# A decoder layer on one core: a ninth slot for expert weights in two halves, and the final gain as one row

## What is computed

```python
def hierarchical_moe(x, g_ffn, w_rg, b_rg, w_re, b_re, w_gate, w_up, w_down):
    xn = rmsnorm(x, g_ffn)
    ...                        # one of 4 groups, then two of its 8 experts, weights in combine
    for g in range(N_EXPERT_GROUPS):
        h = jax.nn.silu(jnp.einsum('nd,edf->nef', xn, w_gate[g])) * jnp.einsum('nd,edf->nef', xn, w_up[g])
        out = out + jnp.einsum('nef,efd->nd', h * combine[:, g, :, None], w_down[g])
    return x + out.reshape(bsz, L, D_MODEL)
...
y_prompt = rmsnorm(h_p, g_final)
y_sample = rmsnorm(h_s, g_final)
```

## Time and profile before

| | us |
|---|---|
| median of 3 runs | 1639.19 |
| lowest and highest of them | 1638.49, 1640.21 |
| the profiled execution, its time | 1643.52 |
| its span, first to last instruction | 1641.7 |
| TensorE busy | 1427.6 (87%) |
| VectorE busy | 531.2 (32%) |
| ScalarE busy | 408.4 (25%) |
| DMA, mean over the span | 332 GB/s, 545.72 MB |

### The profile page before, as it was taken

How to read it: one execution, slowest core, us unless ns; L and a number is a source line. 1 busy time by engine, 2 the same in 40 slices (tenths; PEclk the granted TensorE clock), 3 DMA queues, 4 the chain that set the end, 5 groups by cost and what they waited for, 6 DMA issues and landing times.

```text
span 1641.7 us, 24240 instructions
## 1 busy us (share of the span) xinstructions
PE 1427.6 (87%) x9959; PEld 939.8 (57%) x9959; DVE 531.2 (32%) x840; ACT 408.4 (25%) x684; POOL 26.6 (2%) x48
## 2 busy tenths in 40 slices
PE   7999999999999999998886887877867869958966
PEld 7999999999999999963231321322312412412411
DVE  5547775554455555531110111111111001101103
ACT  6444344333333334420201101101102002002003
POOL 0200020000000000000000000000000000000000
PEclk9999999999999999999898888799889797989979
DMA  8776555555555458589999999999999999999997
GB/s 335 295 259 253 155 161 184 184 184 182 184 179 179 179 217 336 218 308 428 427 429 428 427 429 428 428 428 428 427 428 427 429 428 428 428 429 427 430 428 315
DMA packets 51867, 545.72 MB, mean 332 GB/s; under 512 B 6160, under 2 KB 6208, under 8 KB 11480
## 3 DMA queue, kind: packets, MB, share of 16 engines
q1 hardware_dynamic: 50288, 540.30, 81.2%
q0 software_dynamic: 1392, 4.78, 1.0%
q10 hardware_dynamic: 144, 0.02, 0.0%
HBM read 541.34 MB, written 3.68 MB: 332 GB/s over the span
## 4 chain that ended last, share of the span: by engine, by line
PE 54%; DMA 41%; DVE 2%; ACT 1%; issue 1%; SPq 0%; DVEq 0%; ACTq 0%
DMA side<-in_expert_chunks 23%; DMA ring<-in_expert_chunks 15%; PE bank L1401 11%; PE bank L1402 11%; PE bank L1403 11%; PE bank L1760 8%; PE bank L1669 6%; DMA ring<-in_dense_units 3%; PE bank L1763 2%; PE bank L1697 1%; DVE w_lo L889 1%; ACT w_hi L622 1%; PE bank L1712 0%; PE bank L1563 0%; DMA trunk<-in_mem_cols 0%
## 5 line engine op out<-in xcount | busy, mean ns | idle before, releaser
L889 DVE TENSOR_TENSOR w_lo<-ring,w_hi 128x1024 fp32r<-128x1024 f32 x220 | 259.7, 1221 | 221.5 <-ACT w_hi L622 221.0
L1401 PE MATMUL bank<-xn_hi,w_hi 128*128 128x264 f32 x1120 | 319.8, 286 | 1.6 <-DVE w_lo L889 1.6
L1402 PE MATMUL bank<-xn_lo,w_hi 128*128 128x264 f32 x1120 | 318.1, 284 | 0.0
L1403 PE MATMUL bank<-xn_hi,w_lo 128*128 128x264 f32 x1120 | 317.8, 284 | 0.0
L622 ACT ACTIVATE w_hi<-ring 128x1024 fp32r<-128x1024 f32 x220 | 221.1, 1052 | 371.4 <-PE bank L1403 337.1
L1401 PEld LDWEIGHTS bank<-xn_hi,w_hi 128*128 128x128 f32 x1120 | 211.6, 189 | 3.0 <-issue 1.7
L1402 PEld LDWEIGHTS bank<-xn_lo,w_hi 128*128 128x128 f32 x1120 | 211.8, 189 | 0.1
L1403 PEld LDWEIGHTS bank<-xn_hi,w_lo 128*128 128x128 f32 x1120 | 210.7, 188 | 0.0
L1760 PE MATMUL bank<-ring,trunk 128*32 128x512 f32 x1024 | 144.7, 691 | 64.0 <-DMA ring<-in_expert_chunks 64.0
L1760 PE MATMUL bank<-side,trunk 128*32 128x512 f32 x768 | 122.5, 770 | 58.9 <-DMA side<-in_expert_chunks 58.8
L1669 PEld LDWEIGHTS bank<-trunk,x_all 128*128 128x128 f32 (+1 forms) x780 | 120.4, 211 | 90.0 <-issue 69.4
(11 more groups left out here) (308 smaller groups left out, 1624.4 us busy)
## 6 DMA issues: line engine op xcount, KB each, us to landing
ring<-in_expert_chunks SPq DMA_DIRECT2D x88, 2048.0 KB, 35.6
side<-in_expert_chunks SPq DMA_DIRECT2D x72, 2048.0 KB, 35.5
ring<-in_dense_units SPq DMA_DIRECT2D x109, 1024.0 KB, 4.8
trunk<-in_expert_chunks SPq DMA_DIRECT2D x24, 2048.0 KB, 35.4
ring<-in_expert_chunks SPq DMA_DIRECT2D x16, 1024.0 KB, 34.9
x_all<-in_k_cols SPq DMA_DIRECT2D x8, 512.0 KB, 8.1
x_all<-in_cache_mem_v SPq DMA_DIRECT2D x8, 512.0 KB, 6.7
x_all<-in_x_cols SPq DMA_DIRECT2D x1, 2112.0 KB, 12.1
```

The lines of the kernel that those rows point to most:

```text
L889: V.tensor_tensor(w_lo[n % 2][:, js, :], raw[n % 2][:, js, :], w_hi[n % 2][:, js, :], ALU.subtract).then_inc(lo_done, 1)
L1401: mm(ps[:, 0:n], w_hi[b][:, j, :], x_hi[:, j, :], start=j == k0, stop=False)
L1402: mm(ps[:, 0:n], w_hi[b][:, j, :], x_lo[:, j, :], start=False, stop=False)
L1403: ins = mm(ps[:, 0:n], w_lo[b][:, j, :], x_hi[:, j, :], start=False, stop=j == k1 - 1)
```

## The change

- **A ninth slot.** It consists of two halves in places that were free or have been freed: the place of the broadcast `g_final`, and 2048 words where `y` was. Chunks 14 and 23 of every round go there, each in two loads of 1 MiB. The other slots keep their chunks, but for two: chunk 15 goes to the slot of chunk 6, and chunk 22 to the slot of chunk 7.
- **The order of the loads.** A table `REFILL` says which chunk is loaded when chunk p has been used. In a round the queue now reads 8 to 13, 15, 22, 16 to 21, 23 in halves, then for the next round 6, 0 to 5, 7, and 14 in halves. Before, it read 8 to 23 and then 0 to 7.
- **Ahead of the loop** both halves of chunk 14 are loaded as well, the first where `g_final` was loaded, the second once the router's logits have been folded.
- **`g_final`** is loaded as one row of 8 KiB into partition 64 of the sample rows' tile, early in the output projection. TensorE spreads it to all partitions by a product with a matrix that has one row of ones (`final_gain`): ahead of chunk 17 into bank 0, ahead of chunk 19 into bank 1, ahead of chunk 23 into bank 6, between the halves of chunk 23 into bank 7, in every round. At the end VectorE multiplies from the banks (9 operations of 512 columns in place of 3 of 1536) and copies bank 7 once.
- **`y`** has two buffers of 512 columns in place of four; h is made in place.
- **Sample rows.** The product that puts their last 512 columns in bank 4 uses a shifted identity. It moves from behind the first gather to a place among the busy matmuls, of which two go.

```diff
+SLOT = [EORDER[c % 8] for c in range(CPR)]
+SLOT[14], SLOT[15], SLOT[22], SLOT[23] = 8, SLOT[6], SLOT[7], 8
+REFILL = ([(p, p + 8, 0) for p in range(6)] + [(6, 15, 0), (7, 22, 0)] + [(p, p + 8, 0) for p in range(8, 14)] +
+          [(14, 23, 0), (15, 6, 1)] + [(p, p - 16, 1) for p in range(16, 22)] + [(22, 7, 1), (23, 14, 1)])
...
+        nine_halves = [view(trunk, CHUNK + 2 * D, CHUNK // 2), view(side, 0, CHUNK // 2)]
...
+                    if k == 2:
+                        sp.wait_ge(x_zero, 1)
+                        sp.dma_start(g_row, g_final.rearrange("(o n) -> o n", o=1)).then_inc(gfin_in, 16)
...
-            sp.dma_start(gfin, g_final.rearrange("(o n) -> o n", o=1).to_broadcast([P, D])).then_inc(gfin_in, 16)
+            half_load(14, 0, slice(0, 1))
+            sp.wait_ge(aux_ready, A_LT + 1)
+            half_load(14, 1, slice(0, 1))
...
-            dve.wait_ge(gfin_in, 16)
-            for t, (p0, p1, _, _) in enumerate(ACC):
-                link(V.tensor_tensor(acc(t, 0, 1536), acc(t, 0, 1536), gfin[p0:p1, 0:1536], ALU.mult))
+            for q, signal in ((0, gf_ready), (1, gf_ready), (6, gf2_ready)):
+                dve.wait_ge(signal, npass * ROUNDS)
+                c0 = 512 * min(q, 2)
+                for t, (p0, p1, _, _) in enumerate(ACC):
+                    ins = V.tensor_tensor(acc(t, c0, c0 + 512), acc(t, c0, c0 + 512), bank[q][p0:p1, :], ALU.mult)
+            dve.wait_ge(gf3_ready, npass * ROUNDS)
+            link(V.tensor_copy(g_last, bank[7][:, :]))
...
+                    def final_gain(q, b):
+
+                        return mm(bank[b][:, :], spread_g, x[:, 2, q * 512:(q + 1) * 512], start=True, stop=True)
...
+                        if c == 17:
+                            final_gain(0, 0)
                         if c == 21:
                             last_columns(1)
+                        if c == 19:
+                            final_gain(1, 1).then_inc(gf_ready, 1)
+                        if c == CPR - 1:
+                            pe.wait_ge(aux_done, it * JPR + (A_E + JOB_S[2] + 3))
+                            final_gain(2, 6).then_inc(gf2_ready, 1)
...
                             if jj and c == CPR - 1:
                                 last_columns(2)
+                                final_gain(3, 7).then_inc(gf3_ready, 1)
                                 pe.wait_ge(half_full, it * 16 + 16)
```

More of the change, by code:

```diff
@@ L162, in branch_kernel @@
         fold = view(side, 6 * T, LG)
-        sq_rows = view(side, 7 * T, 3, P)
+        sq_rows = view(side, 6 * T + LG, 3, P)
         at = 4096
@@ L226, in branch_kernel, with weights @@
                   6: view(trunk, 0, CHUNK), 7: view(side, 12544, CHUNK)}
-        y = view(side, 0, 4, 512)
-        hs = view(side, 2048, 512)
-        h = view(side, 2560, 4, P)
+        nine_halves = [view(trunk, CHUNK + 2 * D, CHUNK // 2), view(side, 0, CHUNK // 2)]
+        def weights(s, jj):
+            half = nine_halves[jj] if s == 8 else e_slot[s][:, jj * (CHUNK // 2):(jj + 1) * (CHUNK // 2)]
+            return half.rearrange("p (e n) -> p e n", e=EPR)
+        y = view(side, 2048, 2, 512)
+        hs, h = view(side, 2048, 512), view(side, 2048, 4, P)
         hT = view(side, 3072, 4, P)
-        PwT = view(side, 3584, T)
-        at = 7 * T
+        PwT = view(side, 3784, T)
+        at = 2048
         beats = view(side, at, 192).rearrange("p (t i j) -> p t i j", t=3, i=NE)
@@ L267, in branch_kernel @@
         at += 2
-        assert at <= 3584, at
+        assert at <= 3784, at
         at = 12288
@@ L284, in branch_kernel @@
         Pwf = view(side, at, 3, P)
-        at += 384
+        at += 616
+        shift = view(side, at, S0 + TS)
+        at += S0 + TS
+        spread_g = view(side, at, P)
+        at += P
         assert at <= 17424, at
         acc2 = view(trunk, CHUNK, 2, D)
-        gfin = view(trunk, CHUNK + 2 * D, D)
         xgT = view(trunk, CHUNK + 3 * D, KT, P)
@@ L317, in branch_kernel @@
         smx, snegm, srs = view(small, 224, 1), view(small, 225, 1), view(small, 226, 1)
-        full = [sem(f"slot{i}_full") for i in range(8)]
+        full = [sem(f"slot{i}_full") for i in range(9)]
         mem_in, x_in, xt_in = [sem(f"mem{i}_in") for i in range(4)], [sem("x0_in"), sem("x1_in")], sem("xt_in")
@@ L368, in expert_full, with slot_fills @@
         def expert_full(c):
-            return sum(16 for k in range(c % ESLOTS, c + 1, ESLOTS))
+            return sum(32 if k == 14 else 16 for k in range(c + 1) if SLOT[k] == SLOT[c])
+        def slot_fills(c):
+            return expert_full(max(k for k in range(CPR) if SLOT[k] == SLOT[c]))
         units_v = dense_units.rearrange("m p n -> p m n")
@@ L453, in residual, with half_load @@
                 sp.dma_start(hcol[:, k % HRING:k % HRING + 2, :], x_cols[:, k:k + 2, :]).then_inc(xcol_in[k // 2 % 2], 16)
+            def half_load(c, jj, round_of):
+                sp.dma_start(nine_halves[jj].rearrange("p (o n) -> p o n", o=1),
+                             chunk_v[:, c, round_of, jj * (CHUNK // 2):(jj + 1) * (CHUNK // 2)]).then_inc(
+                                 half_full if c == CPR - 1 and jj else full[8], 16)
             def expert_load(c, round_of):
-                s = EORDER[c % ESLOTS]
-                if c < CPR - 1:
+                s = SLOT[c]
+                if s == 8:
+                    half_load(c, 0, round_of)
+                    half_load(c, 1, round_of)
+                else:
                     sp.dma_start(e_slot[s].rearrange("p (o n) -> p o n", o=1), chunk_v[:, c, round_of, :]).then_inc(full[s], 16)
[L460 to L463, removed]
             for n in range(N_OUT - 6, N_OUT + 16):
@@ L1650, in _ @@
                 mm(bank[2 + t][:, :], ident[:, :], x[:, t, 3 * 512:D], start=True, stop=False)
-            stay_busy(5)
+            pe.wait_ge(shift_ok, 2)
+            mm(bank[4][0:S0 + TS, :], shift[0:TS, :], x[0:TS, 2, 3 * 512:D], start=True, stop=False)
+            stay_busy(3)
             pe.wait_ge(sel_ready, 2)
@@ L1678, in _ @@
             gather(0, 0, 0)
-            pe.wait_ge(acc2_in, 16)
-            mm(bank[4][0:S0 + TS, :], ident[:, 0:S0 + TS], x[:, 2, 3 * 512:D], start=True, stop=False)
+            pe.wait_ge(spread_ok, 2)
+            pe.wait_ge(gfin_in, 16)
             pe.wait_ge(np_ready, 1)
@@ L1696, in scatter_late @@
                         for t, (_, _, t0, cnt) in enumerate(ACC):
-                            mm(bank[2 + t][0:cnt, :], PwT[:, t0:t0 + cnt], y[:, 3, :], start=False,
+                            mm(bank[2 + t][0:cnt, :], PwT[:, t0:t0 + cnt], y[:, 1, :], start=False,
                                stop=True).then_inc(aux_ready, 1)
```

66 lines of the change are left out of this document (38 added, 28 removed).

## The result

The change made the kernel slower, by more than a measurement leaves open. Over 13 runs each the median went from 1637.94 us to 1643.74 us. The ratio is 1.0037, with a 95% interval of 1.0029 to 1.0046, which is 4.8 to 7.5 us. The forecast was +1.05 us, 1640.2, most likely within 0.2%. The time lies in the stated range, but the likeliest case was not the one that came. That it lies there owes something to luck: the forecast stood on a base of 1639.19, and 5.8 us on that base are 1645.0, the very edge of the range.

A forecast was written before the change was run, and what follows sets the result against it. The prediction took DMA bytes at 428 GB/s to bound the loop, plus engine work after the last of them. Its terms, -0.4 and +1.45, sum to +1.05 us on 1639.19, giving 1640.2 us; range 1637.0 to 1645.0.

The forecast's parts named there:

- What bounds the kernel: Pass loop: DMA bytes at 428 GB/s set the steady part; just ahead of the loop and its end are not byte-bound.
- The refill that lands when it did: Chunk 21 of the last round: the 182nd refill before and after, so it lands when it did, less 0.4 us.
- The ninth slot, -4.9: Ahead of the loop: one more chunk preloaded into 3.6 us unused, so the last half lands 4.90 us earlier.
- Halves: Loop loads: eight more chunks loaded as 2 x 1 MiB cost 0.03 us each, 0.2 in all, taken as 0.
- The end, +1.45: Last round: TensorE's ordered work from chunk 21 to 23b takes 11.25 us, before 9.80, so the end moves +1.45 us.
- VectorE at the end: End of the kernel: nine products and the copy are hidden by 1.3 us behind the wait for the square root.
- The start of the loop, -0.4: First expert matmul: without the sample rows' product ahead, chunk 0 starts earlier by 0 to 0.5 us, taken as 0.4.
- a term of +-1.5: First round's chunk 1: half clock could fall later or last longer, +-1.5 us, not predictable.
- TensorE on time at 21, taken as 0: Last round, chunks 16 to 21: TensorE needs 24.2 of 24.5 us, 0.3 spare; lateness taken as 0.
- The rival: Last round's down projection: half clock makes TensorE 5.9 us late at chunk 21, time 1646.1; chance 20%.

The follow-up runs named there:

- e6: Kernel before with only the sample rows' product moved (shifted identity, two busy pairs fewer): ratio 1.0010 to the kernel before.
- e2: Changed kernel plus five additional g_final products ahead of the wait for chunk 16: ratio 1.0024 to the kernel before.
- e9: Changed kernel plus a filling product behind the first gather and five additional products ahead of chunk 16: ratio 1.0013 to the kernel before.
- e4: Changed kernel with chunk 22 loaded behind 21 and the bank 7 product behind the last matmul of chunk 23: ratio 0.9989 to the kernel before.
- e7: Changed kernel with 22 loaded behind 21, bank 7 product behind the last matmul, filling product behind the first gather: ratio 0.9978 to the kernel before.
- e8: As e7, but both halves of the first round's chunk 14 issued only when chunk 0 has been used: ratio 0.9982 to the kernel before.
- e1: Changed kernel with chunk 22 loaded behind chunk 21 again, everything else kept: ratio 1.0002 to the kernel before.
- e5: Changed kernel with a filling product behind the first gather, where the sample rows' product was: ratio 1.0024 to the kernel before.
- e3: Changed kernel without the two g_final products around chunk 23 (banks 6 and 7): ratio 1.0027 to the kernel before.

## Why the prediction was right in part and wrong in part

**What bounds the kernel: right, but for one place.** The steady part is set by DMA at 428 GB/s in both kernels (share 1.01 from 1000 to 1200 us). I named two places that bytes do not bind; the first rounds of refills, with shares of 0.58 to 0.78 in the kernel before, are a third.

**The refill that lands when it did: right, and the best check of the whole reading.** A refill is a load that SyncE issues when TensorE has used a chunk. Chunk 21 of the last round is the 182nd refill in the kernel before, in e6, and in every version with the changed order. In four traces TensorE still waits for this refill. Two are the kernel before and e2 (above). The other two are e6 and e9, whose rows in TensorE's timeline are, in this order:

```profile
1610.73 1.92 PE L1767 MATMUL bank<-ring,side 128*32 128x512 f32 x16 [1.27 <-DMA ring<-in_expert_chunks]
```

```profile
1615.02 1.92 PE L1820 MATMUL bank<-ring,side 128*32 128x512 f32 x16 [1.20 <-DMA ring<-in_expert_chunks]
```

Counted from the first gather, in the order e6, before, e9, e2, these are 903.00, 905.62, 907.12 and 908.04 us. Chunk 2 of the first round started 10.88, 12.53, 14.00 and 15.61 us behind chunk 0 in the same traces. The two series run together: 4.73 us of delay at chunk 2 are 5.04 us at the last refills, some 890 us later. Step by step they agree less well (1.65, 1.47 and 1.61 us at chunk 2 against 2.62, 1.50 and 0.92), and these are four executions, two with eight slots and two with nine. e4 is a further check: its chunk 21 is the 181st refill, waited for DMA and started 902.18 us behind the gather, with chunk 2 at 14.04. One chunk more is 907.08, and e9 has 907.12 with chunk 2 at 14.00. What the start of the loop loses is not won back, since the queue is full from there on.

**The ninth slot, -4.9: right in sign, and right in size as far as the runs tell.** With the end repaired and the start covered (e7) the kernel is 3.6 us faster while 23b is still 0.7 us behind DMA's pace (10.50 us behind chunk 21 where DMA gives 9.80), so the slot is worth about 4.3, good to 1.5 us, which 4.9 is within. I tied it to the 3.6 us unused ahead of the loop; the 0.7 us that e8 lost against e7 on the median, with up to 2.7 inside the error, says that the holes behind chunk 0 can take over part of this or most of it.

**Halves: right.** e7 loads eight more chunks in halves and wins nearly the whole chunk; the spacing of loads that TensorE waits for is 4.90 us in the changed kernel too (1556.07 to 1560.97). At the rate that the Trainium skill ("DMA: Bandwidth & Descriptors", section "Bandwidth") gives for 1 MB they would have cost 10 us more, as an estimate, and the runs do not agree with it for transfers that queue behind one another.

**The end, +1.45: right, a little small.** 11.56 us against the 11.25 of the sum; chunk 21 to 22 took 5.62 for 5.54, and 22 to 23b 5.94 for 5.71. Undoing the order (e1) gave back 5.7 us, where the working gives 4.90 of transfer that count again; the 0.8 between them is within the error of some 2 us.

**VectorE at the end: right.** Hidden by 1.54 us where I had 1.3.

**The start of the loop, -0.4: wrong, in sign too.** This is the step that failed. I read that the copy ends at 715.65 and wrote that the first chunk could start 0.1 us later. It starts 3.26 to 3.30 us behind the gather, with the product or without it; from the end of VectorE's copy to the first matmul it takes 0.6 us here (loading the number of passes and entering two loops lie in between, I haven't parted them). The product had lain in that time and cost nothing. Taking it away left 1.1 us idle and cost 1.6 us by e6, 2.1 by e5. What the idle time does is bring half clock earlier or for longer: in three of the six traces with it chunk 0 itself ran wholly or partly at half clock (2.96 to 3.64 us), in none of the five without it. This fits all five pairs above; it is a count of a few executions, and they overlap. I had named the clock there as a term of +-1.5 that I could not predict, and had not seen that the edit itself moves it.

**TensorE on time at 21, taken as 0: too small.** The working had 24.2 us from 16 to 21 and 0.3 spare. The profile has 24.90, of which 12.61 for chunks 16 to 18 where the working had 11.95, so chunk 21 started 0.4 us late (it landed, by 24.5 us for five chunks, at 1614.84, and started at 1615.24). In the traces of e3 and e5 the same sum gives 0.6 and 0.1 us. By e2 and e9 filling the wait ahead of 16 wins 2.1 and 1.8 us on the median. That the difference is a longer half clock in other executions, as in the sixth round before, is argued only: no profile caught one in a last round. The spread says little. The changed kernel's 13 runs reach over 8.2 us and e7's 11 over 5.3, but the 34 runs of the kernel before beside e1 reach over 8.1 too. The rival named the right place, not the size, which it had at 5.9 us; I gave it 20% and let the forecast keep 0 for it, when the wait ahead of chunk 16 went from 1.4 to 6.3 us.

**The sum again** with what the runs measured: 1.76 for the end (11.56 less 9.80), 1.6 to 2.1 for the start and 2.1 at chunk 16 are 5.5 to 6.0 us, against 5.8. Two of the three terms are differences of medians good to some 2 us each, so that they meet so closely is partly luck, and a further cause of 1 or 2 us could hide in them. The 0.4 us outside the span are such a remainder. The absolute forecast was also 1.25 us high in its base: the median before was 1637.94 over 13 runs, and 1639.19 over the three that I had.

## What to carry to other kernels

When a loop is bound by transfers, read off for each chunk what work must follow it, and load last the chunk with the least work behind it; a chunk pulled ahead in the queue does not move that work, and the bytes saved only count if TensorE is not then the last. An instruction that fills an otherwise idle moment of TensorE costs nothing and may be worth keeping: look at what the engine does in its place before you move it, above all where a queue is paced by that engine. Compare loops from their own first instruction, not by spans, when the part ahead of them varies by more than the effect.

## What the runs showed of the hardware

- Time lost at the start of this transfer-bound loop was still missing at its end. 4.73 us later at chunk 2 were 5.04 us later at the 182nd refill, between the first and the last of four executions.
- An idle stretch of 1.1 us on TensorE ahead of the first chunk, in a part where it is otherwise busy, went with earlier or longer half clock behind it. With the gap chunk 2 came 14.0, 18.3, 15.6, 15.6, 14.0 and 10.9 us behind chunk 0; with it filled 12.5, 14.0, 12.5, 10.9 and 14.0. The means are 14.7 and 12.8 us, and the ranges overlap; it is the medians of the runs (1.6 to 2.1 us in four pairs) that carry the point.
- Five additional products in every round, 4.56 us in the last one, or some 36 us of TensorE in all at that rate, did not make the kernel slower. The medians have it 2.1 us faster (e2) and 1.8 (e9 against e5), the intervals overlapping in both.
